# Spreading projected state-space inputs by DMA through DRAM instead of by identity matmuls, in a two-layer fp32 decoder trunk

## The chip, the cores and the metric

The kernel runs on one core of one Trainium2 chip. The metric is the device time of one execution in microseconds (us). Before the change three runs gave 1001.79, 1001.94 and 1002.18 us; the median is 1001.94 us.

## The reference

The input x is 256 tokens by 1024 channels, fp32. Two layers run one after the other, each a feed-forward block, a mixer and a second feed-forward block, then a final RMSNorm. The mixer of layer 0, the only part that the change touches, is a diagonal state-space model (S5):

```
u = (h @ w_in)                                # 256 tokens x 1024 channels
# 64 groups of 16 channels, each with a 64-dim complex diagonal state
bu = einsum('gph,tgh->tgp', b_bar, u);  s_t = lam_bar * s_(t-1) + bu_t
y  = Re(einsum('ghp,tgp->tgh', c, s)) + d_skip * u
z  = gelu(y);  val, gate = split(z @ w_out);  mixed = val * sigmoid(gate)
```

## The kernel before

Channels lie on the 128 partitions and the 256 tokens on the free axis. Every weight matrix comes as a stream of 326 units of 128 x 1024 numbers. SyncE (the queue SP) loads a unit into one of three `raw` slots (L313), once VectorE has finished with the unit three before it. ScalarE (ACT) rounds it to the high part `w_hi` (L364), VectorE (DVE) makes the low part `w_lo` (L803), in rings of four, and TensorE (PE) multiplies high by high, high by low and low by high (L1299 to L1301). The rounding of a unit waits, by `unit_done`, until PE has used the unit four before it. PE, ACT and DVE each follow an order written out by hand; nothing overtakes on an engine, and the engines meet by semaphores.

The S5 mixer starts with unit `b` of the stream (`b = S5_BASE`). Units b to b+7 project the input, one for every 128 channels, into the four PSUM banks of `acc`: bank q holds units 2q and 2q+1, 256 channels, and is called quarter q. The recurrence is not run token by token. The 256 tokens are cut into 64 chunks of 4 steps. For it the inputs have to lie with 4 steps x 32 channels (two groups, a pair) on the 128 partitions and with 8 pairs x 64 chunks on the free axis. That is the tile `u`, of which quarter q has 128 x 512 numbers. How one quarter runs:

- `inputs(q)`: ACT copies bank q from PSUM to the SBUF buffer `own_u` (L598), step-major. `own_u` has two halves, q even and q odd. ACT waits for the second unit of the quarter, and for q = 2 and 3 until PE has read the half that it overwrites.
- `s5_move(q)`: PE multiplies 16 blocks of 128 x 32 of the identity by `own_u` and so brings each step and each block of 32 channels to its partitions, back in bank q (L1617).
- `s5_scale_u(q)`: DVE multiplies bank q by the reciprocal RMS by steps, `rstd_step`, and writes `u` (L1052).
- `s5_inflow(q)`: PE multiplies `u` by the input matrices of the states, into the banks `gu` or `mx` (L1630).
- `s5_scan(q)`: DVE turns the inflow by tables (L1073 to L1079) and scans it over the chunks, real and imaginary part (L1082).
- `s5_state(q)`: DVE turns it back and writes the real part over `u` and the imaginary part to `state_im` (L1091 to L1101).
- `s5_own(q)`: PE computes what a chunk's inputs give in the chunk itself (L1638); `s5_outflow(q)`: PE adds what the states give (L1654). Then ACT applies gelu (L618), PE turns z back (L1663), and the output projection starts with `value_gate` (L1694).

In the code of the mixer, `project(k)` is the projection by unit b+k, and `split_after(n)` is the split of unit n+4: on ACT its rounding, on DVE its low part. The order of PE after unit 2 is: inflow(0), project(3), own(0), move(1), project(4), inflow(1), project(5), own(1), move(2), outflow(0), project(6), inflow(2), project(7), own(2), move(3), outflow(1), inflow(3), own(3), the turns of quarters 0 and 1, outflow(2), two corrections, value_gate parts, outflow(3). DVE runs scan(q), scale_u(q+1), state(q), with the low parts of two units after state(0), of one after state(1) and of none after state(2). ACT runs inputs(1), the roundings of b+7 and b+8, inputs(2), those of b+9 and b+10, inputs(3), that of b+11.

Of the kernel before, what the change touches and what calls it, by code (L numbers as in the profile page):

```python
# [62 lines left out]
CH = 2 * GROUP  # L63
STEPS = 4
CHUNKS = SEQ // STEPS
QUARTERS = 4
# [34 lines left out]
def trunk(nc, x_in, gains, last_gain, wstream, lam_re, lam_im, log_dt, b_re, b_im, c_re, c_im, skip, out):  # L101
    with ExitStack() as ctx:
# [3 lines left out]
        def sem(name):  # L106
            return ctx.enter_context(nc.semaphore(name))
# [112 lines left out]
        toep_act, toep_dve = sem("toep_act"), sem("toep_dve")  # L220
        rot_started, rot_ready, decay_ready = sem("rot_started"), sem("rot_ready"), sem("decay_ready")
        u_copied, u_moved, turned_back = sem("u_copied"), sem("u_moved"), sem("turned_back")
        rotated, unrotated, state_cleared = sem("rotated"), sem("unrotated"), sem("state_cleared")
        zeroed, skip_ready, own_done = sem("zeroed"), sem("skip_ready"), sem("own_done")
        u_ready, inflow_done, inflow_read = sem("u_ready"), sem("inflow_done"), sem("inflow_read")
# [72 lines left out]
        def last_turn(m, i):  # L298

            return isinstance(i, int) and i == TURNS - 1 and m == BODY - 1  # L300

        block = ctx.enter_context(nc.Block())

# [52 lines left out]
        def _(act):  # L356
# [9 lines left out]
            def split_after(done):  # L366

                if done + RING < UNITS:
                    n = done + RING
                    split_hi(n, n % RAW, n % RING)  # L370
# [219 lines left out]
            def s5_mixer():  # L590
                b = S5_BASE
                def inputs(q):
                    act.wait_ge(unit_done, b + 2 * q + 2)
                    if q == 0:
                        act.wait_ge(rot_ready, 1)
                    if q >= 2:
                        act.wait_ge(u_moved, q - 1)
                    act.activation(own_u[:, q % 2].rearrange("p t (j c) -> p t c j", j=STEPS),  # L598
                                   acc[:, q, :].rearrange("p (t c j) -> p t c j", t=2, j=STEPS),
                                   ACT.Copy).then_inc(u_copied, 1)  # L600

                inputs(0)
                root_by_steps(1)
# [1 line left out]
                split_after(b + 1)  # L605
                split_after(b + 2)
                inputs(1)
                split_after(b + 3)
                split_after(b + 4)
                inputs(2)  # L610
                split_after(b + 5)
                split_after(b + 6)
                inputs(3)
                split_after(b + 7)

                def gelu(q):
                    act.wait_ge(y_done, q + 1)
# [173 lines left out]
        def _(dve):  # L791
# [256 lines left out]

            def s5_scale_u(q):

                dve.wait_ge(u_moved, q + 1)
                dve.tensor_tensor(u[:, QP * q:QP * (q + 1), :], acc[:, q, :].rearrange("p (a c) -> p a c", a=QP),  # L1052
                                  rstd_step[:, :].unsqueeze(1).broadcast_to([P, QP, CHUNKS]),
                                  ALU.mult).then_inc(u_ready, 1)

# [237 lines left out]
        def _(pe):  # L1293
# [316 lines left out]
            def s5_move(q):  # L1610

                pe.wait_ge(u_copied, q + 1)
                for i in range(4):
                    for j in range(STEPS):
                        dst = acc[CH * j:CH * (j + 1), q, :].rearrange("p (t i c) -> p t i c", t=2, i=4)[:, :, i, :]
                        src = own_u[:, q % 2, :, CHUNKS * j:CHUNKS * (j + 1)]
                        mm = pe.matmul(dst, ident[:, CH * i:CH * (i + 1)], src, start=True, stop=True)  # L1617
                mm.then_inc(u_moved, 1)
# [81 lines left out]
            def s5_mixer():  # L1700
# [11 lines left out]
                s5_inflow(0)  # L1712
                project(3)
                s5_own(0)
                s5_move(1)
                project(4)
                s5_inflow(1)
                project(5)
                s5_own(1)
                s5_move(2)  # L1720
                s5_outflow(0)
                project(6)
                s5_inflow(2)
                project(7)
                s5_own(2)
                s5_move(3)
                s5_outflow(1)
                s5_inflow(3)
                s5_own(3)
# [471 lines left out]
```

## Time and profile before

| | |
|---|---|
| median of three runs | 1001.94 us |
| profiled execution, first to last instruction (span) | 999.6 us |
| what lies around the span, by the difference to the median | 2.3 us |
| PE busy | 987.1 us, 99% |
| DVE busy | 744.5 us, 74% |
| ACT busy | 571.2 us, 57% |
| moved by DMA | 172.57 MB, mean 173 GB/s |
| mean granted TensorE clock | 0.999 |

The page gives no other time for the profiled execution than its span; the difference to the median of the runs, 2.3 us, is taken as what lies around it. PE is the matmul engine; PEld in a row is its weight load, which overlaps. A queue's name with a q behind it (SPq, ACTq) is the issuing of DMAs by that engine. In the rows, `s_memory` is the block of SBUF that holds `u`, `own_u`, `state_im` and the tables, and `low_part` and `mx`, `gu`, `acc` are what the code calls them. A time in a timeline is microseconds from the span's start.

### The profile page before, as it was taken

The page shows a single profiled execution, that of the slowest core. Times are in us where ns is not written, and L with a number is a line of the kernel's source. Part 1 is how long each engine was busy: PE and PEld are TensorE (multiplying, and loading weights), DVE is VectorE, ACT ScalarE, POOL GpSimd, SP SyncE. Part 2 cuts the span into 40 slices and gives each one's busy share as a digit, 9 for nine tenths or more (in the row PEclk, how much of TensorE's full clock was granted, in tenths as well). Part 3 has the DMA queues.
Part 4 walks back from the last instruction along what each step waited for, and adds up shares of the span by engine and source line. Part 5 has one row for each costly group of instructions (what it writes and reads, how often), then busy time and mean ns, then how long its engine had stood idle before and what let it go on. Part 6 is the DMA issues. An engine that isn't in the chain of part 4 may idle for free.

```text
span 999.6 us, 19015 instructions
## 1 busy us (share of the span) xinstructions
PE 987.1 (99%) x7304; PEld 904.0 (90%) x7304; DVE 744.5 (74%) x922; ACT 571.2 (57%) x794; POOL 114.4 (11%) x144
## 2 busy tenths in 40 slices
PE   8999999999999999999999999999999999999997
PEld 8999999989999888888898888888899898888886
DVE  5789986889976777777687777776566587666666
ACT  7444447573365655555465555555599765555555
POOL 4854138100001000000010000001000010000000
PEclk9999999999999999999999999999999999999999
DMA  7555555443075565666646666566544256655563
GB/s 253 192 174 183 170 177 164 149 132 121 23 218 184 183 196 185 190 183 191 196 148 214 189 188 190 184 180 193 186 126 125 85 154 218 190 192 188 190 190 108
DMA packets 49049, 172.57 MB, mean 173 GB/s; under 512 B 6097, under 2 KB 6097, under 8 KB 48977
## 3 DMA queue, kind: packets, MB, share of 16 engines
q1 hardware_dynamic: 48544, 170.99, 54.3%
q8 instruction: 54, 0.88, 0.4%
q10 hardware_dynamic: 432, 0.55, 0.2%
q14 instruction: 19, 0.15, 0.0%
HBM read 170.47 MB, written 1.05 MB: 172 GB/s over the span
## 4 chain that ended last, share of the span: by engine, by line
PE 73%; DVE 13%; POOL 6%; ACT 4%; issue 4%; DMA 1%; SPq 0%; DVEq 0%; POOLq 0%; ACTq 0%
PE mx L1314 11%; PE gu L1314 11%; PE mx L1317 6%; PE gu L1317 6%; PE acc L1356 4%; PE gu L1299 4%; PE gu L1300 4%; PE gu L1301 4%; DVE w_lo L803 4%; PE acc L1360 2%; PE gu L1356 2%; PE mx L1356 2%; PE acc L1343 2%; PE acc L1345 2%; PE acc L1347 2%
## 5 line engine op out<-in xcount | busy, mean ns | idle before, releaser
L803 DVE TENSOR_TENSOR w_lo<-raw,w_hi 128x1024 fp32r<-128x1024 f32 x258 | 324.3, 1266 | 91.0 <-ACT w_hi L364 90.4
L364 ACT ACTIVATE w_hi<-raw 128x1024 fp32r<-128x1024 f32 x259 | 270.5, 1052 | 80.8 <-DMA raw<-wstream_dram 22.3
L1299 PE MATMUL gu<-g,w_hi 128*128 128x256 f32 x560 | 161.4, 288 | 1.5 <-DVE g L943 1.3
L1300 PE MATMUL gu<-g,w_hi 128*128 128x256 f32 x560 | 158.4, 283 | 0.0
L1301 PE MATMUL gu<-g,w_lo 128*128 128x256 f32 x560 | 158.4, 283 | 0.0
L1314 PE MATMUL mx<-g,w_hi 128*128 128x512 f32 x480 | 119.9, 392 | 0.0
L1314 PE MATMUL gu<-g,w_hi 128*128 128x512 f32 x464 | 116.2, 392 | 0.0
L1299 PEld LDWEIGHTS gu<-g,w_hi 128*128 128x128 f32 x560 | 107.3, 192 | 2.3 <-issue 1.5
L1300 PEld LDWEIGHTS gu<-g,w_hi 128*128 128x128 f32 x560 | 107.4, 192 | 0.1
L1301 PEld LDWEIGHTS gu<-g,w_lo 128*128 128x128 f32 x560 | 107.3, 192 | 0.0
L1314 PEld LDWEIGHTS mx<-g,w_hi 128*128 128x128 f32 x480 | 87.0, 189 | 16.0
L1314 PEld LDWEIGHTS gu<-g,w_hi 128*128 128x128 f32 x464 | 83.8, 188 | 15.6
L374 ACT ACTIVATE tmp<-tmp 128x256 f32<-128x256 f32 x68 | 28.4, 418 | 108.8 <-DVE tmp L813 86.6
L1940 POOL TENSOR_TENSOR ssq<-ssq,tmp 128x512 f32<-128x512 f32 x12 | 18.5, 1538 | 583.6 <-ACT tmp L510 583.6
L877 DVE TENSOR_TENSOR w_lo<-raw,w_hi 128x1024 fp32r<-128x1024 f32 x58 | 70.8, 1223 | 16.2 <-ACT w_hi L479 16.2
L1317 PEld LDWEIGHTS mx<-g,w_lo 128*128 128x128 f32 x480 | 65.5, 190 | 4.7
L1317 PEld LDWEIGHTS gu<-g,w_lo 128*128 128x128 f32 x464 | 63.2, 190 | 4.7
L1317 PE MATMUL mx<-g,w_lo 128*128 128x256 f32 x480 | 66.9, 282 | 0.0
L479 ACT ACTIVATE w_hi<-raw 128x1024 fp32r<-128x1024 f32 x57 | 60.0, 1053 | 11.1 <-PE mx L1317 5.1
L1317 PE MATMUL gu<-g,w_lo 128*128 128x256 f32 x464 | 64.6, 282 | 0.0
L820 DVE TENSOR_TENSOR tmp<-tmp 128x256 f32<-128x256 f32 x88 | 40.5, 460 | 12.3 <-ACT tmp L374 11.6
L1299 PE MATMUL acc<-h_hi,w_hi 128*128 128x256 f32 x168 | 48.4, 288 | 0.1
(309 smaller groups left out, 1927.1 us busy)
## 6 DMA issues: line engine op xcount, KB each, us to landing
raw<-wstream_dram SPq DMA_DIRECT2D x318, 512.0 KB, 3.7
x<-x_in_dram SPq DMA_DIRECT2D x4, 256.0 KB, 5.9
raw<-wstream_dram SPq DMA_DIRECT2D x3, 256.0 KB, 5.7
out_dram<-x_tok SPq DMA_DIRECT2D x3, 256.0 KB, 2.0
gain_row<-last_gain_dram SPq DMA_DIRECT2D x1, 512.0 KB, 4.4
raw<-wstream_dram ACTq DMA_DIRECT2D x1, 256.0 KB, 4.6
s_memory<-b_re_dram SPq DMA_DIRECT2D x1, 256.0 KB, 4.6
s_memory<-b_im_dram SPq DMA_DIRECT2D x1, 256.0 KB, 5.2
```

The source lines that it names most:

```text
L364: act.activation(weights(unit)[0], raw[:, s_raw, :], ACT.Copy).then_inc(hi_ready, 1)
L374: act.activation(tmp[:, f % 2, 2, :], tmp[:, f % 2, 0, :], ACT.Silu).then_inc(silu_ready, 1)
L479: act.activation(w_hi[:, n0 % RING, :], raw[:, n0 % RAW, :], ACT.Copy).then_inc(hi_ready, 1)
L803: dve.tensor_tensor(lo, raw[:, n % RAW, :], hi.bitcast(F32), ALU.subtract).then_inc(lo_ready, 1)
L820: dve.tensor_tensor(tmp[:, m, 3, :], tmp[:, m, 2, :], tmp[:, m, 1, :], ALU.mult).then_inc(h_ready, 1)
L877: dve.tensor_tensor(w_lo[:, n0 % RING, :], raw[:, n0 % RAW, :], w_hi[:, n0 % RING, :].bitcast(F32), ALU.subtract).then_inc(lo_ready, 1)
L1299: pe.matmul(dst, a, hi, start=start, stop=False, skip_group_check=check)
L1300: pe.matmul(dst, a, lo, start=False, stop=False, skip_group_check=check)
L1301: return pe.matmul(dst, b_, hi, start=False, stop=stop, skip_group_check=check)
L1314: pe.matmul(bank.rearrange("p (r t) -> p r t", r=2), w_hi[:, s, P * kb:P * kb + P], g_both[:, :, kb, :], start=kb == 0, stop=False, skip_g ...
L1317: last = pe.matmul(bank[:, 0:SEQ], w_lo[:, s, P * kb:P * kb + P], g_hi[:, kb, :], start=False, stop=kb == KB - 1, skip_group_check=True)
L1356: pe.matmul(kept_bank(d).rearrange("p (i t) -> p i t", i=2), w_hi[:, s, at:at + P], h_kept[:, 2 * p + r, :, :], start=p == 0 and r == 0, s ...
```

## The change

Quarter 0 stays as it is. For quarters 1, 2 and 3 the identity matmuls (`s5_move`) go. ACT, after its copy to `own_u`, issues four DMAs that write 32 partitions each to a DRAM scratch `u_dram` (64 KB each, in runs of 64 numbers, 256 bytes). Two roundings later (one, in quarter 3) it waits until all four have landed (`u_stored`), and issues one DMA that reads the quarter back (256 KB, 128 rows of 2 KB) straight into `u`. DVE then waits for that DMA (`u_spread`) and multiplies `u` in place, from SBUF instead of from PSUM. The wait before `inputs(3)` is for the stores of quarter 1; that before `inputs(2)` stays a wait on PE's move of quarter 0.

```diff
+        u_dram = nc.dram_tensor("u_dram", (QUARTERS, STEPS, CH, 2, 4, CHUNKS), F32, kind="Internal").ap()
@@ scalar engine, s5_mixer
                     act.wait_ge(unit_done, b + 2 * q + 2)
                     if q == 0:
                         act.wait_ge(rot_ready, 1)
-                    if q >= 2:
-                        act.wait_ge(u_moved, q - 1)
+                    if q == 2:
+                        act.wait_ge(u_moved, 1)
+                    if q == 3:
+                        act.wait_ge(u_stored[1], 16 * 4)
+                def store_inputs(q):
+                    act.wait_ge(u_copied, q + 1)
+                    for i in range(4):
+                        rows = slice(CH * i, CH * (i + 1))
+                        act.dma_start(u_dram[q, :, :, :, i, :].rearrange("j h t c -> h t j c"),
+                                      own_u[rows, q % 2].rearrange("p t (j c) -> p t j c", j=STEPS)).then_inc(
+                            u_stored[q], 16)
+
+                def spread_inputs(q):
+                    act.wait_ge(u_stored[q], 16 * 4)
+                    act.dma_start(u[:, QP * q:QP * (q + 1), :].rearrange("p a c -> p (a c)"),
+                                  u_dram[q].rearrange("j h t i c -> (j h) (t i c)")).then_inc(u_spread[q], 16)
                 inputs(1)
+                store_inputs(1)
                 split_after(b + 3)
                 split_after(b + 4)
+                spread_inputs(1)
                 inputs(2)
+                store_inputs(2)
                 split_after(b + 5)
                 split_after(b + 6)
+                spread_inputs(2)
                 inputs(3)
+                store_inputs(3)
                 split_after(b + 7)
+                spread_inputs(3)
@@ vector engine
             def s5_scale_u(q):
-                dve.wait_ge(u_moved, q + 1)
-                dve.tensor_tensor(u[:, QP * q:QP * (q + 1), :], acc[:, q, :].rearrange("p (a c) -> p a c", a=QP),
+                mine = u[:, QP * q:QP * (q + 1), :]
+                if q:
+                    dve.wait_ge(u_spread[q], 16)
+                else:
+                    dve.wait_ge(u_moved, 1)
+                dve.tensor_tensor(mine, mine if q else acc[:, q, :].rearrange("p (a c) -> p a c", a=QP),
                                   rstd_step[:, :].unsqueeze(1).broadcast_to([P, QP, CHUNKS]),
@@ tensor engine, s5_mixer
                 s5_own(0)
-                s5_move(1)
                 project(4)
                 s5_inflow(1)
                 project(5)
                 s5_own(1)
-                s5_move(2)
                 s5_outflow(0)
                 project(6)
                 s5_inflow(2)
                 project(7)
                 s5_own(2)
-                s5_move(3)
                 s5_outflow(1)
```

## Rows read from the trace of the kernel before

**Rows 1.** Page, part 1: busy time (share of the span) and instructions.

```profile
PE 987.1 (99%) x7304; PEld 904.0 (90%) x7304; DVE 744.5 (74%) x922; ACT 571.2 (57%) x794; POOL 114.4 (11%) x144
```

**Rows 2.** Waits of PE, longest first: total us, times, longest us.

```profile
PE gu L1299 <- DVE g L943: 1.3, 1, 1.3
```

**Rows 3.** Windows: length, busy us by engine, granted clock, DMA share, GB/s.

```profile
229.28:273.03 43.75, 43.09 (x642) 40.04 (x642) 43.42 (x59) 15.30 (x18) 0.00 (x0) 1.00 0.18 59
```

**Rows 4.** Chain that ended last, in the S5 mixer: start us, us, what.

```profile
258.81 0.59 DVE s_memory L1052
...
259.45 2.09 PE mx L1630 x64
...
273.24 1.95 PE acc L1654 x32
```

**Rows 5.** Source line L1617, the moves: duration ns min/median/max, first and last start.

```profile
L1617 PE MATMUL acc<-s_memory,ident x128: 272/273/297, 224.5 to 257.1; 128*32 128x128 f32 x128
```

**Rows 6.** Timeline of PE: start us, us, line, operation [idle before <-releaser].

```profile
232.22 1.09 PE L1638 MATMUL acc<-s_memory 128*64 128x128 f32 x16
233.49 1.08 PE L1617 MATMUL acc<-s_memory,ident 128*32 128x128 f32 x32 [0.17 <-ACT s_memory L598]
...
234.50 0.39 PE L1299 MATMUL acc<-g,w_hi 128*128 128x256 f32 x1
...
237.56 0.34 PE L1630 MATMUL mx<-s_memory,low_part 128*64 128x64 f32 x4
...
249.91 0.34 PE L1630 MATMUL gu<-s_memory,low_part 128*64 128x64 f32 x4
...
257.27 2.02 PE L1654 MATMUL acc<-s_memory 128*64 128x128 f32 x32
```

**Rows 7.** Timeline of ACT, the copies (L598) and roundings (L364).

```profile
232.33 1.10 ACT L598 ACTIVATE s_memory<-acc 128x512 f32<-128x512 f32 x1 [1.02 <-PE acc L1301]
...
237.72 1.06 ACT L364 ACTIVATE w_hi<-raw 128x1024 fp32r<-128x1024 f32 x1 [3.43 <-PE acc L1301]
242.74 1.10 ACT L598 ACTIVATE s_memory<-acc 128x512 f32<-128x512 f32 x1 [3.96 <-PE acc L1301]
...
250.08 1.06 ACT L364 ACTIVATE w_hi<-raw 128x1024 fp32r<-128x1024 f32 x1 [4.13 <-PE acc L1301]
255.10 1.10 ACT L598 ACTIVATE s_memory<-acc 128x512 f32<-128x512 f32 x1 [3.96 <-PE acc L1301]
256.49 1.06 ACT L364 ACTIVATE w_hi<-raw 128x1024 fp32r<-128x1024 f32 x1 [0.29 <-DMA raw<-wstream_dram]
```

**Rows 8.** Timeline of DVE: the first multiply into u, the last state.

```profile
235.06 0.67 DVE L1052 TENSOR_TENSOR s_memory<-acc,rstd_step 128x512 f32<-128x512 f32 x1
...
272.35 0.68 DVE L1101 TENSOR_TENSOR s_memory<-tmp 128x504 f32<-128x504 f32 x1
```

**Rows 9.** Page, part 6, DMA issues: count, KB each, median us to landing.

```profile
raw<-wstream_dram SPq DMA_DIRECT2D x318, 512.0 KB, 3.7
...
out_dram<-x_tok SPq DMA_DIRECT2D x3, 256.0 KB, 2.0
...
s_memory<-b_re_dram SPq DMA_DIRECT2D x1, 256.0 KB, 4.6
```

**Rows 10.** Source lines L748 and L331: what one DMA issue takes, ns min/median/max.

```profile
L748 ACTq DMA_DIRECT2D raw<-wstream_dram x1: 450/450/450, 1.3 to 1.3; - x1
...
L331 SPq DMA_DIRECT2D par<-lam_im_dram x1: 712/712/712, 5.3 to 5.3; - x1
```

**Rows 11.** Source line L324, three 256 KB loads at the kernel's start: issue, landing.

```profile
L324 SPq DMA_DIRECT2D raw<-wstream_dram x3: 388/432/432, 0.8 to 3.1; - x3
...
DMA to landing us min/median/max: 2.8/5.7/6.6
```

**Rows 12.** Windows at the kernel's end, columns as in Rows 3.

```profile
993.00:994.00 1.00, 0.61 (x3) 0.19 (x1) 0.93 (x4) 0.91 (x3) 0.00 (x0) 1.00 0.00 0
...
997.00:998.00 1.00, 0.00 (x0) 0.00 (x0) 0.00 (x0) 0.00 (x0) 0.00 (x0) 0.69 0.70 272
```

More of the change, by code:

```diff
@@ L222, in trunk @@
         u_copied, u_moved, turned_back = sem("u_copied"), sem("u_moved"), sem("turned_back")
+        u_stored = [sem(f"u_stored{q}") for q in range(QUARTERS)]
+        u_spread = [sem(f"u_spread{q}") for q in range(QUARTERS)]
         rotated, unrotated, state_cleared = sem("rotated"), sem("unrotated"), sem("state_cleared")
```

## The prediction, made before the changed kernel ran

> **What bounds the kernel now.** I read the page's busy shares first. PE is busy 987.1 of 999.6 us [rows 1], and the longest wait of any PE group is 1.3 us [rows 2]. So elsewhere in the kernel nothing that is late in the mixer can be made good: what the mixer loses, the kernel loses. The change touches only the stretch from about 232 to 260 us, and the windows show that from 229.28 to 273.03, 43.75 us, PE is busy 43.09 and DVE 43.42 us [rows 3]. Two engines are full at once, at the full clock (1.00, the 2.4 GHz level), so a saving on one alone is worth next to nothing. Which of them sets the end the chain tells: it runs through DVE up to the multiply into `u` of quarter 3 at 258.81, and only then over inflow(3) at 259.45 to outflow(3) at 273.24 [rows 4]. DVE's last state write ends at 273.03 [rows 8], 0.2 us before outflow(3) starts. Both routes meet there.
>
> **What goes.** Each move is 32 matmul records that start within about 1 us [rows 5, 6]. With the wait for ACT's copy before it, it costs more: own(0) starts at 232.22 and project(4) at 234.50 [rows 6], 2.28 us, of which own itself takes about 1.0 (1.09 with the drain of its last matmul). So each move is worth 1.3 us of PE's time, three 3.9 us. DVE saves nothing: it multiplies the same 128 x 512 numbers; from SBUF instead of PSUM I take the same 0.67 us [rows 8].
>
> **What comes.** Per quarter ACT issues five DMAs, and the inputs make two trips one after the other, each with its landing waited for.
> - One issue: 0.45 us on ACT's queue [rows 10], 0.71 us for the slowest of small rows [rows 10]. I take 0.45, the row of the same queue: four stores hold ACT 1.8 us, and the last starts 1.35 us after the first.
> - A store's landing: 256 KB in 2 KB rows to DRAM land in 2.0 us [rows 9]. The new ones are a quarter of that in 256-byte runs; bounds 1.5 (fewer bytes; three quarters of that row) and 3.5 us (near the 3.7 of a 512 KB load [rows 9]). I take 2.0.
> - The read back, 256 KB: the quickest load of this size landed in 2.8 us [rows 11], one among other loads took 4.6 [rows 9], and a store of the size 2.0 [rows 9]. The DMA engines are at 0.18 in this stretch [rows 3] and the weight queue is held up by DVE's late splits, so I take 2.8; bounds 2.0 and 4.2 (short of the 4.6, which stood in a row of loads).
>
> On DMA: Bandwidth & Descriptors (Specifications) in the Trainium skill speaks against the change: below 512 bytes a transfer is read, modified and written. No row of this trace shows a store in such runs. If it brought the landing to the 3.5 us bound, two of the three quarters would wait longer, by 2.6 us in all.
>
> Nothing else hides in the edit: the wait of `inputs(3)` on the stores of quarter 1 has long been met, and PE and DVE issue no DMA.
>
> **The sum, quarter by quarter.** Queued behind the new wait on DVE are state(q-1), the low parts and scan(q); behind ACT's wait for the stores is the next `inputs`; PE sits in inflow(q).
> - Quarter 1. The copy ends at 233.43 [rows 7]. Stores are issued from 233.55 to 235.35 and landed at 236.9. ACT then rounds b+7 until 236.35. Project(4) runs 1.3 us earlier, so the rounding of b+8, at 237.72 before [rows 7], is free to start at 236.4 and ends at 237.4. The read back is issued there and lands at 240.2; DVE multiplies until 240.9, against a start at 235.06 before [rows 8]; inflow(1) starts at 241.0 against 237.56 [rows 6]: 3.45 us late. PE, finished with project(4) at 236.15, is idle for 4.85 us.
> - Quarter 2. From inflow(1) to the copy of quarter 2 it is 242.74 - 237.56 = 5.2 us [rows 6, 7], so that copy starts at 246.2. The stores land at 250.7, but in front of the read back stands the rounding of b+10, which waits for project(6): 250.08 - 237.56 = 12.5 us after inflow(1) [rows 6, 7], 11.2 without the move. That is 252.2; rounded at 253.2, read back issued at 253.3, landed at 256.1, multiplied at 256.8. inflow(2) starts at 256.85 against 249.91 [rows 6]: 6.95 late, after 4.85 us of idle PE.
> - Quarter 3. The copy follows 5.2 us after inflow(2) [rows 6, 7]: 262.05 to 263.15. Last store issued 264.6, landed 266.6; the rounding of b+11 waits for its load as it did before [rows 7] and ends at the same time, 266.6. Read back issued 266.7, landed 269.5, multiplied 270.25; inflow(3) at 270.3 against 259.45 [rows 4]: 10.85 late. PE ends outflow(1) about 264.9 (2.02 us from 257.27 before [rows 6], shifted by 6.95 and less the last move), so it idles 5.4 us.
> - After it. inflow(3) to outflow(3) was 13.8 us of full PE [rows 4], and stays so: 284.1. By DVE: multiply at 269.6, then state(2), scan(3), state(3), 273.03 - 258.81 = 14.2 us before [rows 4, 8], gives 283.8. Both routes end 10.8 us late.
>
> So without a change of the clock the span goes to 999.6 + 10.85 = 1010.4, and with the 2.3 us around it the time to 1012.8. The check: 15.1 us of new idle PE less 3.9 of moves is 11.2.
>
> **The clock.** PE is idle three times for about 5 us. The only such stretch in the trace is the end: PE stops in 993 to 994 (0.61 us busy), and in 997 to 998 the granted clock is 0.69 of full [rows 12], that is, it fell to the 1.2 GHz level after some 4 us without a matmul. My three gaps are 0.8 to 1.3 us longer than that. One sample says that a fall can come in each, not that it must; I give each a chance a little under even, 1.3 falls of three. What follows the gap, an inflow of 2.1 us and a projection of 2.9, would take twice as long at the lower level until it rises: up to 4.9 us more, 2.5 if it rises halfway. I take 2.4 per fall, and 1.3 of them: 3.2 us. The three gaps stay on the path to the next copy, so this adds in full.
>
> On the clock, TensorE: Matmul & The Clock Gate (Why this matters for your kernels) in the Trainium skill warns against idle gaps between bursts of matmuls, after which the array is back at half rate. The row of the end agrees; by that rule alone all three gaps would cost, 7.2 us instead of 3.2.
>
> Forecast: 1012.8 + 3.2 = 1016.0 us.
>
> **The rivals.**
> - The clock stays up: 1012.8. For it: the gaps exceed the one sample by only about a microsecond. Range 1010 to 1015 with the bounds of the read back.
> - Dear transfers: store at 3.5 (+2.6) and read back at 4.2 (+1.4 each, 4.2), with two falls: 1012.8 + 6.8 + 4.8 = 1024.4. For it: short runs and small rows have no price in this trace. Against it: the DMA engines are nearly free here.
> - The transfers are hidden, no change: 1001.9. It would need copy end to multiply within what there is now, 235.06 - 233.43 = 1.6 us in quarter 1 [rows 7, 8], where one landing alone is 2.0. Even then DVE's full queue keeps the end.
> - Faster: PE, not DVE, is what the end hangs on. Then the 3.9 us of moves come back: 998.0. It decides where a quarter's two trips fit in 1.6 us and DVE gives up 3.9 us that it doesn't give in rows 3. Both speak against it.
>
> **How the numbers follow.** Forecast (chain exposed, one or two falls) 0.50; clock stays up 0.27; dear transfers or three falls 0.17; hidden 0.03; faster 0.03. The range is 1010.5 to 1023.0: below it lie the two last rivals and a read back of 2.0 us, above it the far end of the dear case. Slower by over 0.2% (2 us, about what a measurement of this kernel can tell from no change) is 0.50 + 0.27 + 0.17 = 0.94, within it 0.03, faster 0.03.
>
> **What would show it.** In the profile after: DVE's multiply L1052 (its line after) waiting for the read-back DMA three times, by about 5.1, 3.5 and 2.2 us; inflow idle before by 4.9, 4.9 and 5.4 us; five issues per quarter on ACTq at 0.45; landings of 2.0 and 2.8 us; granted clock below 1.00 somewhere in 240 to 280; nothing lost or won after the mixer. I am wrong if ACT's issues or the short runs cost twice what I take, or if DVE waits but PE makes it good from other work.

## The result

| | before | after |
|---|---|---|
| median of five runs | 1001.94 us | 1018.97 us |
| lowest and highest | 1001.44, 1002.55 | 1015.86, 1022.58 |
| profiled execution, span | 999.6 us | 1014.1 us |
| mean granted clock of the profiled execution | 0.999 | 0.994 |

The ratio is 1.0168, with a 95% interval of 1.0149 to 1.0187: the kernel became 17 us slower. Forecast were 1016.0 us and a range of 1010.5 to 1023.0. Two things are worth reading in the table. The profiled execution, at 1015.86 us, is the quickest of the five, so its trace shows less of the loss than the median has. And the five runs lie 6.7 us apart, where those of before lie 1.1 us apart. The mean granted clocks of the five are 0.994, 0.993, 0.992, 0.990 and 0.988 in the order of their times, quickest first: 6 us of missing clock (0.006 of 1017 us) between the ends, for 6.7 us of time. (Five runs are few for a spread: 21 later runs of the kernel before lay 3.0 us apart.)

The page of after, busy shares and DMA issues (KB each, median us to landing):

```profile
PE 989.0 (98%) x7208; PEld 906.8 (89%) x7208; DVE 745.1 (73%) x922; ACT 571.5 (56%) x794; POOL 114.4 (11%) x144
...
u_dram<-s_memory ACTq DMA_DIRECT2D x12, 64.0 KB, 2.3
s_memory<-u_dram ACTq DMA_DIRECT2D x3, 256.0 KB, 2.5
```

PE has 96 instructions less than in [rows 1] and 1.9 us more of busy time, since a matmul at the lower clock is busy for longer: inflow(1) took 3.59 us in the chain of after, an inflow at the full clock 2.09 [rows 4]. DVE and ACT do the same work as before. What is new is waiting. The waits of after in the stretch 225 to 300 us, longest first (total us, times, longest us):

```profile
DVE s_memory L1081 <- DMA s_memory<-u_dram: 12.6, 3, 5.4
PEld mx L1659 <- DVE s_memory L1081: 11.1, 2, 6.0
PE mx L1659 <- DVE s_memory L1081: 10.7, 2, 5.7
...
PE gu L1659 <- DVE s_memory L1081: 3.3, 1, 3.3
```

L1081 is the multiply into `u`, L1052 before; L1659 is the inflow, L1630 before. DVE waits three times for the read-back, 12.6 us in all, and behind it PE waits 14.0 us. The timeline of ACT and its queue in after (start us, us):

```profile
232.33 1.10 ACT L604 ACTIVATE s_memory<-acc 128x512 f32<-128x512 f32 x1 [2.78 <-PE acc L1330]
233.46 3.09 ACTq L612 DMA_DIRECT2D u_dram<-s_memory  x4
236.65 2.00 ACT L368 ACTIVATE w_hi<-raw 128x1024 fp32r<-128x1024 f32 x2 [3.22 <-PE acc L1330]
238.04 0.35 ACTq L618 DMA_DIRECT2D s_memory<-u_dram  x1
248.02 1.10 ACT L604 ACTIVATE s_memory<-acc 128x512 f32<-128x512 f32 x1 [9.38 <-PE acc L1330]
249.16 3.06 ACTq L612 DMA_DIRECT2D u_dram<-s_memory  x4
252.32 1.06 ACT L368 ACTIVATE w_hi<-raw 128x1024 fp32r<-128x1024 f32 x1 [3.19 <-issue]
253.97 1.06 ACT L368 ACTIVATE w_hi<-raw 128x1024 fp32r<-128x1024 f32 x1 [0.59 <-PE acc L1330]
253.99 0.33 ACTq L618 DMA_DIRECT2D s_memory<-u_dram  x1
263.88 1.11 ACT L604 ACTIVATE s_memory<-acc 128x512 f32<-128x512 f32 x1 [8.85 <-PE acc L1330]
265.02 2.56 ACTq L612 DMA_DIRECT2D u_dram<-s_memory  x4
```

The first copy starts at the very time of [rows 7]. One trip round is a copy (1.1 us), four issues (3.1), the landing, one issue, another landing, the multiply, inflow, project, and the next copy. Before, the copies came 10.4 and 12.4 us after each other [rows 7], now 15.7 and 15.9. The multiplies on DVE in after, and its last state write:

```profile
240.58 0.69 DVE L1081 TENSOR_TENSOR s_memory<-s_memory,rstd_step 128x512 f32<-128x512 f32 x1 [5.43 <-DMA s_memory<-u_dram]
256.46 0.69 DVE L1081 TENSOR_TENSOR s_memory<-s_memory,rstd_step 128x512 f32<-128x512 f32 x1 [3.37 <-DMA s_memory<-u_dram]
271.64 0.69 DVE L1081 TENSOR_TENSOR s_memory<-s_memory,rstd_step 128x512 f32<-128x512 f32 x1 [3.79 <-DMA s_memory<-u_dram]
...
285.29 0.69 DVE L1130 TENSOR_TENSOR s_memory<-tmp 128x504 f32<-128x504 f32 x1
```

and outflow(3) in the timeline of PE:

```profile
287.47 2.02 PE L1683 MATMUL acc<-s_memory 128*64 128x128 f32 x32
```

DVE's last state write begins at 285.29 against 272.35 [rows 8], 12.94 us late, and 12.6 of that are the three waits. On PE outflow(3) begins at 287.47; in the chain of after it stands at 287.54, 14.3 us after its place in the chain of before [rows 4]. So PE is 1.4 us later than DVE is. Before, outflow(3) followed 0.2 us behind the end of DVE's last state write, now 1.6 us behind it (285.98 to 287.54): from inflow(3) to outflow(3) PE takes 15.2 us (272.38 to 287.54), where it took 13.8 before [rows 4]. From outflow(3) on almost nothing is lost or won: the spans differ by 14.5 us. Windows of after (columns as in [rows 3]) show where the 1.4 us come from:

```profile
240.00:242.00 2.00, 0.67 (x12) 0.68 (x14) 1.42 (x2) 0.00 (x0) 0.00 (x0) 0.82 0.06 22
242.00:244.00 2.00, 2.00 (x44) 2.00 (x42) 1.99 (x5) 0.00 (x0) 0.00 (x0) 0.50 0.00 0
244.00:246.00 2.00, 2.00 (x29) 1.93 (x26) 1.97 (x3) 0.00 (x0) 0.00 (x0) 0.83 0.00 0
...
258.00:260.00 2.00, 2.00 (x47) 1.88 (x41) 1.99 (x5) 0.00 (x0) 0.00 (x0) 0.59 0.00 0
260.00:262.00 2.00, 2.00 (x10) 2.00 (x11) 1.97 (x4) 0.00 (x0) 0.00 (x0) 0.56 0.04 8
...
272.00:274.00 2.00, 1.61 (x30) 1.62 (x32) 1.99 (x4) 0.00 (x0) 0.00 (x0) 0.50 0.00 0
274.00:276.00 2.00, 2.00 (x48) 2.00 (x46) 1.97 (x4) 0.00 (x0) 0.00 (x0) 0.65 0.01 4
```

Behind each of PE's three gaps, of 4.9, 3.3 and 5.7 us, the granted clock is at the 1.2 GHz level for a while. The missing share of it comes to 1.7 us each time (0.36 + 1.00 + 0.34 in the first), 5.1 us in all. The last of the three stands between inflow(3) and outflow(3), and is what makes that stretch 1.4 us longer. Not all of the 5.1 us is time lost: a fall costs only where nothing else is waited for.

### The profile page after: what moved, and what is told of

The parts are those of the page before. It is cut to its first block, busy times and chain, and to the rows that moved or that the text cites. A ratio compares the mean times of both kernels' runs of the same rounds, so it can differ in the third digit from the quotient of the medians.

```text
span 1014.1 us, 18838 instructions
## 1 busy us (share of the span) xinstructions
PE 989.0 (98%) x7208; PEld 906.8 (89%) x7208; DVE 745.1 (73%) x922; ACT 571.5 (56%) x794; POOL 114.4 (11%) x144
## 4 chain that ended last, share of the span: by engine, by line
PE 81%; DVE 7%; POOL 3%; ACT 3%; issue 2%; DMA 1%; ACTq 0%; SPq 0%; DVEq 0%; POOLq 0%
PE mx L1343 11%; PE gu L1343 11%; PE mx L1346 6%; PE gu L1346 5%; PE gu L1328 5%; PE gu L1330 5%; PE gu L1329 5%; PE acc L1385 4%; DVE w_lo L828 3%; PE acc L1389 2%; PE gu L1385 2%; PE mx L1385 2%; PE acc L1372 2%; PE acc L1374 2%; PE acc L1376 2%
```

## The experiments

Each kernel was timed beside runs of the kernel before on the same chip, and the ratios are against those. My theory was a chain: DVE's full queue sets the end of the stretch, so what DVE waits for the two landings is lost one for one, and to that comes the clock that falls in PE's gaps. (An idle-time matmul, or filler, below is a matmul whose result nobody reads.)

**One quarter alone.** The change for quarter 1; quarters 2 and 3 are moved by PE as before.

```diff
-                store_inputs(2)
-                spread_inputs(2)
-                store_inputs(3)
-                spread_inputs(3)
                 s5_own(1)
+                s5_move(2)
...
                 s5_own(2)
+                s5_move(3)
```

> The change for quarter 1 alone; quarters 2 and 3 are moved by PE as before. Theory (VectorE's queue is the bound, so its wait is lost one for one and PE's slack beside it is not): VectorE waits 5.4 us once and is full from there on, and the time is 5.4 to 6.5 us above the kernel before, about 1007.5 us. Rival (PE's lateness counts, 3.5 us in quarter 1 less what PE has saved): 1004.5 to 1005.5 us.

Measured: 1007.82 us, ratio 1.0054 (1.0039 to 1.0070), 5.7 us above the median of before beside it. The multiplies on DVE in this kernel:

```profile
241.09 0.69 DVE L1077 TENSOR_TENSOR s_memory<-s_memory,rstd_step 128x512 f32<-128x512 f32 x1 [5.84 <-DMA s_memory<-u_dram]
253.52 0.67 DVE L1077 TENSOR_TENSOR s_memory<-acc,rstd_step 128x512 f32<-128x512 f32 x1
264.79 0.67 DVE L1077 TENSOR_TENSOR s_memory<-acc,rstd_step 128x512 f32<-128x512 f32 x1
```

One wait of 5.84 us, none for a DMA after it, and the time is up by 5.7. PE's lateness in that quarter, less by what it saved, would have been smaller, so the rival as it stands fell. The time alone does not shut out PE, though: the granted clock in this kernel is 0.59 and 0.56 from 240 to 248 us, 3.4 us of missing clock, and PE's wait of 5.4 us, less the move and with a part of that, comes out near 5.7 too. What shows that the wait of DVE is lost is DVE's own timeline, where the last state write begins at 278.42, 6.1 us late; outflow(3) can't run before it.

**No moves, and nothing in their place.**

```diff
                 s5_own(0)
-                s5_move(1)
...
-                dve.wait_ge(u_moved, q + 1)
+                if q:
+                    dve.wait_ge(u_copied, q + 1)
+                else:
+                    dve.wait_ge(u_moved, 1)
```

> The kernel before without the identity matmuls of quarters 1 to 3 and with no DMA in their place: VectorE multiplies the bank as the projection left it, after ScalarE's copy. This leaves out the spreading of three quarters, so the numbers that it computes are others; only the time is of use. It is the change with transfers that cost nothing. Theory (VectorE's full queue sets the end of the stretch): three moves are 3.9 us of PE, but PE then waits in front of outflow(3), and the time is 1001.0 to 1002.0 us, at most 1 us less than before. Rival (PE sets the end): 998.0 us.

Measured: 1002.67 us, ratio 1.0003 (0.9993 to 1.0012). That is 0.7 us above the range of the theory, and far from the rival's 998.0. The 3.9 us of PE work that the change takes away are worth nothing, even with transfers that cost nothing. I had expected the wait in front of outflow(3); it stands in front of inflow(3), the longest wait of PE in this kernel (total us, times, longest us):

```profile
PE mx L1633 <- DVE s_memory L1055: 3.3, 1, 3.3
```

and in the window behind it (columns as in [rows 3]):

```profile
260.00:264.00 4.00, 4.00 (x76) 3.95 (x72) 3.85 (x7) 0.55 (x2) 0.00 (x0) 0.57 0.02 6
```

PE waits in front of inflow(3) for what it has saved, and behind that wait the clock is at 0.57 for 4 us. That is 1.7 us of clock lost by doing less work, and here it costs time: DVE's last state write is only 0.2 us late (272.56), outflow(3) 1.8 us (274.95 against 273.17 in PE's timeline). Only this execution has a trace; by their mean clocks it happened in half of the ten runs: five have 0.995 or 0.996 and took 1002.95 to 1004.84 us, the others 0.999 or 1.000 and 1001.18 to 1002.39. Even the five runs at the full clock have a median only 0.3 us below that of the kernel before beside them (1002.42).

**The DMAs beside the moves, read by nobody.**

```diff
+                    if q > 1:
+                        act.wait_ge(u_spread[q - 1], 16)
-                    act.dma_start(u[:, QP * q:QP * (q + 1), :].rearrange("p a c -> p (a c)"),
+                    act.dma_start(h_lo[:, :, :].rearrange("p k t -> p (k t)").bitcast(F32),
...
                 norm_block(2, KB - 1)
+                act.wait_ge(u_spread[3], 16)
```

> The kernel before with its moves, and beside them all the DMAs of the change: ScalarE issues the twelve stores and the three read-backs at the places of the change, but the read-backs go to a tile that nobody reads, and VectorE multiplies the moved bank as before. It prices the issues, ScalarE's wait for the stores and the traffic by themselves. Theory (only VectorE's wait for the landing costs): 1001.9 to 1003 us. Rival (ScalarE's queue, held for 2.5 to 3.1 us by the issues and longer by the wait for the stores, makes roundings late, or the short runs slow the weight stream): 1005 us or more.

Measured: 1004.95 us, ratio 1.0022 (1.0013 to 1.0032). That is 2.2 us by the ratio and 2.5 by the medians, above the theory's 1003 and just short of the rival's 1005: the theory fell, and the rival's cause, ACT's held queue, is seen, though not at the roundings. DVE's last state write is on time in this kernel (272.46). But ACT's queue holds the first gelus behind the stores of quarter 3. The timeline of ACT in this kernel (start us, us):

```profile
256.35 3.75 ACTq L612 DMA_DIRECT2D u_dram<-s_memory  x4
...
261.58 0.33 ACTq L620 DMA_DIRECT2D h_lo<-u_dram  x1
261.94 1.28 ACT L645 ACT_TABLE_LOAD   x1 [0.69 <-DMA u_dram<-s_memory]
263.24 1.09 ACT L645 ACTIVATE s_memory<-acc 128x512 f32<-128x512 f32 x2
```

and PE's own timeline at that place:

```profile
263.89 1.14 PE L1691 MATMUL acc<-ident,s_memory 128*128 128x128 f32 x8 [1.37 <-ACT s_memory L645]
```

PE stands 1.4 us before it can turn z, in a stretch where it was full. In the changed kernel this does not show: the inflow of quarter 3 is later still, and nothing waits for the gelus there.

The rest need not be the price of the DMAs. The edit has one wait more, at the end of the mixer, and behind it ACT's next table load comes late (timeline of ACT):

```profile
325.16 1.28 ACT L392 ACT_TABLE_LOAD   x1 [4.34 <-issue]
```

In the kernel before, this table load starts as soon as ACT's last activation of the mixer ends (at 319.37). The read-back that the new wait is for had been issued at 261.58, so why the load is late is not shown. PE then waits 1.9 us in all for DVE's `h_kept`, which it never does in the kernel before. The profiled execution is one of the slower ones (1005.91), and its outflow(3) is 1.6 us late of 4.5 us in the span. So 2.2 us is an upper bound for the traffic and the issues; 1.4 of it has a place in the trace.

**PE kept busy in the gaps.**

```diff
+            def s5_fill(q, n):
+
+                pe.wait_ge(neg_ready, 1)
+                if q >= 2:
+                    pe.wait_ge(inflow_read, q - 1)
+                for _ in range(n):
+                    pe.matmul((gu, mx)[q % 2][:, 0, 0:SEQ], neg_ident[:, :], g_hi[:, 0, :], start=True, stop=True,
+                              skip_group_check=True)
...
                 project(4)
+                s5_fill(1, 38)
                 s5_inflow(1)
...
                 project(6)
+                s5_fill(2, 24)
                 s5_inflow(2)
...
                 s5_outflow(1)
+                s5_fill(3, 44)
                 s5_inflow(3)
```

> The changed kernel, with idle-time matmuls on PE in front of inflow(1), inflow(2) and inflow(3): 38, 24 and 44 matmuls of 128x256 at 0.118 us each, into the PSUM bank that the inflow overwrites. They give PE work for 4.5, 2.8 and 5.2 us of the waits and change nothing else. Theory (the loss is made of a chain of DMA trips, and of the clock that falls in the gaps): the granted clock stays at 1.00, the three stretches of 3.4 us at the lower level go, each worth 1.7 us of PE work, and the time is about 1011 us (1018.97 before; the profiled execution of 1015.86 less 5), with runs that lie closer together than the 6.7 us of the changed kernel. Rival (the clock costs nothing on the path, the scatter has another source such as the DMAs): 1015 to 1019, scatter as before. Second rival (the fillers run past the landing of the inputs and delay the inflow): above 1019.

Measured: 1015.53 us, 1013.93 to 1016.34, ratio 1.0131 (1.0116 to 1.0147). The scatter shrinks from 6.7 us in five runs to 2.4 in four, and the time by 3.4 us by the medians, 3.7 by the ratios, whose intervals do not touch; so the clock does cost, but the 1011 us that I expected are missed by 4.5. Windows around quarter 2 in this kernel:

```profile
252.00:256.00 4.00, 3.63 (x31) 3.43 (x30) 1.57 (x2) 1.06 (x1) 0.00 (x0) 1.00 0.38 109
256.00:260.00 4.00, 2.71 (x70) 2.64 (x71) 3.45 (x6) 0.00 (x0) 0.00 (x0) 1.00 0.02 6
```

and the timeline of ACT and its queue there:

```profile
246.98 1.11 ACT L604 ACTIVATE s_memory<-acc 128x512 f32<-128x512 f32 x1 [7.91 <-PE acc L1330]
...
253.19 1.06 ACT L368 ACTIVATE w_hi<-raw 128x1024 fp32r<-128x1024 f32 x1 [1.33 <-DMA raw<-wstream_dram]
254.00 0.33 ACTq L618 DMA_DIRECT2D s_memory<-u_dram  x1
```

The clock stays at 1.00 and the copy of quarter 2 comes 1 us sooner than in the changed kernel, yet its read-back is issued at 254.00, as before at 253.99. The gain was taken within one quarter by something that the clock doesn't drive. Two candidates stand in these rows: the rounding in front of the read-back, which waits for its weight load, or the stores' own landing. The four stores of quarter 2 decide it for this execution (source line L612, window 240 to 258; ns, then us to landing):

```profile
L612 ACTq DMA_DIRECT2D u_dram<-s_memory x4: 577/630/649, 248.1 to 250.1; - x4
DMA to landing us min/median/max: 3.6/3.9/4.0
```

The rounding began at 253.19, so it was out of the way; the last store was issued at 250.1 and took 3.9 us to land, which is 254.0. In the changed kernel the same four took 2.5 to 2.8 us.

With the clock at 1.00 this kernel is also the cleanest sight of the bound: DVE waits 11.8 us for the read-backs, its last state write is 12.5 us late (284.87), so is outflow(3) (285.67 in PE's timeline), and the span is 12.5 us longer than before.

**The read-back in front of the roundings**, in the changed kernel and together with the fillers.

```diff
                 store_inputs(2)
+                spread_inputs(2)
                 split_after(b + 5)
                 split_after(b + 6)
-                spread_inputs(2)
```

> The changed kernel with one thing moved: on ScalarE the read-back of a quarter is issued as soon as its four stores have landed, in front of the one or two roundings of weight units instead of behind them. Theory (the landing of the stores comes last anyway: they are issued over 2.6 to 3.1 us and land 2.1 to 2.3 us after the last issue): nothing gained, within 1 us of the changed kernel, 1017 to 1020 us. Rival (my prediction's step for quarter 2, that the rounding which waits for project(6) holds the read-back): 2 to 3 us less, 1015 to 1017 us.

> The changed kernel with both edits: idle-time matmuls on PE in the three gaps, and the read-back issued ahead of the roundings. In the profile with the fillers alone the copy of quarter 2 came 1 us earlier than in the changed kernel, but the read-back was issued at the same time, because the rounding in front of it waited for its weight load. Theory (what the steady clock gave was taken by the order of ScalarE's queue): with both, 1 to 2 us less than with the fillers alone, 1013.5 to 1014.5 us. Rival (the stores land that late by themselves, since the weight load runs beside them): as with the fillers alone, 1015 to 1016 us.

Measured: without fillers 1017.32 us, ratio 1.0154 (1.0141 to 1.0168), an interval that overlaps that of the changed kernel; with fillers 1014.99 us, ratio 1.0127 (1.0112 to 1.0143), against 1.0131 without the move. Neither differs from its partner by more than the intervals allow. Both runs moved the read-back in all three quarters (the cut shows quarter 2). The stores of quarter 2 in the first of these kernels say why (timeline of ACT and its queue):

```profile
249.34 2.58 ACTq L612 DMA_DIRECT2D u_dram<-s_memory  x4
255.39 0.33 ACTq L618 DMA_DIRECT2D s_memory<-u_dram  x1
```

The read-back is issued as soon as the stores allow, and the slowest of them takes 4.1 us from its issue to its landing (the median of this quarter is 2.7); with fillers the four take 4.0 to 4.1. So what took the gain of the clock is the landing of the stores, not the order of ACT's queue; the theory that both edits together win fell, its rival holds. A weight load of 512 KB is in flight beside these stores (issued at 247.9 in the first kernel, landed 6.7 us later); in quarter 3 of that kernel, where the load issued at 263.9 had landed before the last store was issued at 268.4, all four take 2.1. So late landings go together with loads in flight in these traces; no run separates the two.

**Short runs in the loads instead of in the stores.**

```diff
-        u_dram = nc.dram_tensor("u_dram", (QUARTERS, STEPS, CH, 2, 4, CHUNKS), F32, kind="Internal").ap()
+        u_dram = nc.dram_tensor("u_dram", (QUARTERS, P, 2, STEPS, CHUNKS), F32, kind="Internal").ap()
...
+                    act.dma_start(u_dram[q].rearrange("p t j c -> p (t j c)"),
+                                  own_u[:, q % 2].rearrange("p t n -> p (t n)")).then_inc(u_stored[q], 16)
...
+                    for j in range(STEPS):
+                        act.dma_start(
+                            u[CH * j:CH * (j + 1), QP * q:QP * (q + 1), :].rearrange("p (t i) c -> p t i c", t=2),
+                            u_dram[q].rearrange("(i h) t j c -> j h t i c", i=4)[j]).then_inc(u_spread[q], 16)
```

> The changed kernel with the short runs moved from the stores to the loads: one store per quarter writes the copy as it lies, 128 rows of 2 KB, and four loads of 32 partitions read it back in runs of 256 bytes. Bytes, trips and waits are the same. Theory (what counts is two landings one after the other and five issues on one queue, wherever the short runs are): four issues of 0.6 to 0.7 us now stand behind the wait for the store instead of in front of it, and the time is that of the changed kernel, 1016 to 1021 us. Rival (stores in runs below 512 bytes are dear in themselves, loads are not): the store lands sooner by 1 us or more and the chain gets shorter by 1 us a quarter, 1013 to 1016 us.

Measured: 1020.79 us, ratio 1.0180 (1.0166 to 1.0194). Its DMA issues:

```profile
u_dram<-s_memory ACTq DMA_DIRECT2D x3, 256.0 KB, 2.9
s_memory<-u_dram ACTq DMA_DIRECT2D x12, 64.0 KB, 2.3
```

The time is within the theory's range, and the rival (the store lands 1 us sooner, 1013 to 1016 us) fell. A store of 256 KB in 2 KB rows landed in 2.9 us at the median, a quarter of the bytes in 256-byte runs in 2.3 in the page of after: the short writes are not what is dear. The long rows do not land early in quarter 2 either: that store took 3.8 us, the one of quarter 3 2.0. The Trainium skill says, in DMA: Bandwidth & Descriptors (Specifications), that transfers below 512 bytes are read, modified and written. Whether that happened no trace here can show; a cost of it is not seen in the landings. What is dear is the issuing. One plain store or load is issued in 0.33 to 0.35 us, a DMA of 32 partitions and 256 runs in 0.58 to 1.07 in the changed kernel.

**Work put over the trips.** Three kernels with the projections ahead of the inflows. The first sends all three quarters by DMA, the second only quarters 2 and 3 (quarter 1 is moved by PE, and DVE keeps its order, the last three lines of the cut), the third adds 20 idle-time matmuls to the second in front of inflow(3). The read-backs of quarters 1 and 2, where they are, stand one rounding earlier.

```diff
                 project(4)
-                s5_inflow(1)
                 project(5)
+                s5_inflow(1)
                 s5_own(1)
                 s5_outflow(0)
                 project(6)
-                s5_inflow(2)
                 project(7)
+                s5_inflow(2)
...
-                s5_scale_u(1)
                 s5_state(0)
+                s5_scale_u(1)
```

> All three quarters by DMA as in the change, but with work put over the trips: PE runs project(5) before inflow(1) and project(7) before inflow(2), so that the copies of quarters 2 and 3 and their trips start early; VectorE runs state(0) before it multiplies quarter 1; the read-back stands one rounding earlier. Theory (the loss was the exposed trips alone): VectorE waits only once, 1.6 to 2 us for quarter 1, and the time is 1003 to 1006 us. Rival (the DMAs cost something besides VectorE's wait, or the gaps of PE only move and the clock still falls): 1008 us or more.

> As the reordered kernel, but only quarters 2 and 3 go by DMA; quarter 1 is moved by PE as before and VectorE keeps its order. Theory: no wait of VectorE is left, two moves (2.6 us of PE) are gone, VectorE's full queue still sets the end, and the time is that of the kernel before, 1001.5 to 1003.5 us; what PE saves stands as a wait in front of inflow(3), where the clock can fall as it did with no moves at all. Rival: PE's saving is worth something, 999.5 us.

> The same with 20 idle-time matmuls (2.4 us) on PE in front of inflow(3). Theory: the granted clock stays at 1.00 there, and the time is 0.5 to 1 us below the one without them and nowhere below the kernel before by more than 0.5 us: 1001 to 1002.5 us. Rival (the wait in front of inflow(3) is harmless): no difference between the two.

Measured: 1010.60 us, ratio 1.0083 (1.0069 to 1.0097); 1007.86 us, ratio 1.0061 (1.0048 to 1.0075); 1008.24 us, ratio 1.0060 (1.0046 to 1.0074). The first wins back half of the loss, but all three theories are missed by 4 to 6 us. The first one's rival, 1008 us or more, holds; the third is no quicker than the second, as its rival says, though its fillers did not cover the wait. DVE's waits for the read-back had indeed shrunk to 3.6 and 2.8 us. What I had not seen stands in the timeline of ACT and its queue, here of the second kernel:

```profile
253.64 3.09 ACTq L610 DMA_DIRECT2D u_dram<-s_memory  x4
261.20 1.06 ACT L368 ACTIVATE w_hi<-raw 128x1024 fp32r<-128x1024 f32 x1 [7.59 <-DMA raw<-wstream_dram]
261.21 0.33 ACTq L616 DMA_DIRECT2D s_memory<-u_dram  x1
```

Now that the copies come early, the rounding in front of the read-back waits 7.6 us for a weight load, and the read-back with it. The stores before it had landed by 258.2 (the last issued at 256.1, 2.1 us), so here it was the order that held the read-back, for 3.0 us. The PE gap in front of inflow(3) had grown to 6.3 us, more than 20 fillers cover, and the clock fell in both kernels (0.80 from 256 to 264 and 0.77 from 264 to 272 in the second, 0.92 and 0.65 in the third).

**The same, mended.** Read-backs ahead of the roundings, 50 fillers in front of inflow(3).

> The kernel with two quarters by DMA and work over the trips, mended at the two places that its profile shows: the read-backs are issued ahead of the roundings that waited for weight loads, and 50 idle-time matmuls instead of 20 stand in front of inflow(3). Theory (nothing but exposed landings and the clock made it slow): VectorE's waits shrink below 1 us in all and the time is 1002 to 1004 us. Rival (the stores land late beside the weight loads, 3.4 us in that profile, so quarter 2 stays exposed by 2 us): 1005 to 1007 us. Neither is below the kernel before.

Measured: 1006.48 us, ratio 1.0045 (1.0032 to 1.0059), and the rival holds. The granted clock is 1.00 from 252 to 276 us, so nothing of the 4.4 us is the clock. Quarter 3 is hidden, quarter 2 is not, as DVE's timeline shows:

```profile
251.81 0.69 DVE L1077 TENSOR_TENSOR s_memory<-s_memory,rstd_step 128x512 f32<-128x512 f32 x1 [3.15 <-DMA s_memory<-u_dram]
263.11 0.67 DVE L1077 TENSOR_TENSOR s_memory<-s_memory,rstd_step 128x512 f32<-128x512 f32 x1
```

**Quarter 3 alone, hidden.** PE moves quarters 1 and 2, project(7) runs before inflow(2), and the read-back goes ahead of the rounding.

```diff
                 project(6)
-                s5_inflow(2)
                 project(7)
+                s5_inflow(2)
                 s5_own(2)
...
                 store_inputs(3)
+                spread_inputs(3)
                 split_after(b + 7)
-                spread_inputs(3)
```

> The change for quarter 3 alone, with its trips hidden: quarters 1 and 2 are moved by PE, project(7) runs before inflow(2), so that the copy of quarter 3 comes 3 us before its place in the kernel before, and the read-back is issued ahead of the rounding. In the kernel with two quarters by DMA this quarter's inputs lay ready 3 us before VectorE asked for them. Theory (a hidden transfer is worth nothing, since VectorE's full queue and not PE sets the end; its exposed time is all that it costs): VectorE waits 0 to 1 us, the time is that of the kernel before, 1001.5 to 1003.5 us. Rival (PE's move was worth its 1.3 us): 1000.5 to 1001 us. Second rival (ScalarE's held queue makes the gelus late, as with the DMAs that nobody reads): 1004 us.

Measured: 1005.49 us, ratio 1.0034 (1.0022 to 1.0045). The theory is missed by 2 us, and both rivals lie below what was measured. DVE never waits for a DMA in it, and still it waits, as its timeline shows:

```profile
255.36 1.22 DVE L1096 TENSOR_TENSOR tmp<-gu,s_memory 128x1024 f32<-128x1024 f32 x1 [1.89 <-PE gu L1653]
261.29 0.69 DVE L1075 TENSOR_TENSOR s_memory<-s_memory,rstd_step 128x512 f32<-128x512 f32 x1
```

and the window in which PE waits for it:

```profile
260.00:266.00 6.00, 3.97 (x74) 3.97 (x76) 5.80 (x10) 2.53 (x4) 0.00 (x0) 0.72 0.11 38
```

Putting project(7) in front of inflow(2) to start the trip early makes scan(2) wait 1.89 us for the inflow, and PE, ahead of DVE after that, waits 4.0 us in front of inflow(3), where the clock falls again. The trip is hidden, and making room for it costs 3.6 us by the medians. The new order was not run without the DMAs, so how much of that is the order's alone is not shown. No kernel here that sends inputs by DMA is as quick as the one before.

## Why the prediction was right, and where its terms were off

- **The bound.** Held, as long as the clock is up. With the moves gone and no transfers the ratio is 1.0003 (0.9993 to 1.0012); with the gaps filled DVE waits 11.8 us and everything is 12.5 us late. Where the clock falls behind the last gap it is PE that reaches outflow(3) last: 1.4 us behind DVE's lateness in the changed kernel. The check by PE's account comes out as well: 14.0 us of new waits less 3.9 of moves is 10.1, and 4.2 of the 5.1 us of missing clock bring it to 14.3.
- **The issues.** Mis-sized. I took 0.45 us each, 1.8 for four stores, by the row of a load of 128 rows [rows 10]; they took 3.1, 3.1 and 2.6 us. The last store starts 2.5, 2.0 and 1.9 us after the first instead of 1.35, which makes a quarter 0.6 to 1.1 us longer wherever the stores come last. The upper row, 0.71, was the better neighbour.
- **The landings.** The last stores of quarters 1 and 3 landed in 2.1 us (taken: 2.0), the read-backs in 2.4 to 2.5 (taken: 2.8); both errors are small and opposed. The stores of quarter 2 took 2.5 to 2.8 us in the changed kernel, and up to 4.1 in its variants. I had called the DMA engines free by their mean share over 44 us, 0.18 [rows 3]; while these stores run, from 248 to 252 us, it is 0.77 in the changed kernel, their own bytes included.
- **Quarter 1.** Multiply at 240.58, forecast 240.2 to 240.25; inflow(1) at 241.33, forecast 241.0. Right to 0.4 us by two errors that cancel: the stores landed at 238.0 (forecast 236.9), behind the roundings instead of in front of them, and the read-back took 0.3 us less.
- **Quarter 2.** Multiply at 256.46, forecast 256.1; inflow(2) at 257.21, forecast 256.85. Right to 0.4 us, and that is luck. The copy came at 248.02, 1.8 us later than forecast (246.2), since inflow(1) and project(5) ran in part at the lower clock. I let the read-back wait for the rounding behind project(6), and it did: the rounding begins at 253.97, the read-back at 253.99. But it waited for the rounding's start and not, as I had it, for its end 1.1 us later, and the landing was 0.4 us shorter; these two made up for most of PE's lateness. The stores, which I had landed at 250.7, landed at about 253.6 (the last issued at 251.1, 2.5 us). So the order that I blamed held the read-back by 0.3 us only, and with the rounding out of the way the time doesn't measurably change. It did hold it where the copies came early.
- **Quarter 3.** Multiply at 271.64, forecast 269.6; inflow(3) at 272.38, forecast 270.3. Of these 2.1 us 1.8 stand already at the copy (263.88, forecast 262.05): 0.4 come from quarter 2, and from inflow(2) to the copy PE takes 6.7 us where I took 5.2, by the clock that falls behind gap 2. The longer issues add 0.6, the quicker read-back takes 0.3 off.
- **The waits.** DVE waited 5.4, 3.4 and 3.8 us for the read-backs, forecast 5.1, 3.5 and 2.2; PE stood 4.9, 3.3 and 5.7 us, forecast 4.9, 4.9 and 5.4. Gap 2 is shorter than forecast because project(6), at the end of a stretch that the clock had slowed, came later.
- **The clock.** I gave 1.3 falls of 2.4 us each, 3.2 us. (1.3 times 2.4 is 3.1.) The profiled run has three, with 1.7 us of missing clock each. That they add in full did not hold: the first is swallowed by gap 2, as inflow(2) is only 0.4 us late; the second costs 1.5 us up to the copy of quarter 3, the third 1.4 on the way to outflow(3), 2.9 us together. Filling the gaps gives 3.4 us back at the median (1.0168 to 1.0131), and 1.9 between the two profiled runs (1015.86 and 1013.93), each the quickest of its kernel. So the size was about right by luck: more falls, each smaller, one of them free. The Trainium skill's warning about idle gaps, in TensorE: Matmul & The Clock Gate (Why this matters for your kernels), held for all three gaps of this run; that all three falls would cost in full, 7.2 us, did not.
- **The sum.** Forecast 1012.8 without falls and 1016.0 with them. The kernel with its gaps filled, whose clock stays at 1.00 in the mixer, has 1015.5: the chain was undersized by about 2.5 us at the median, and by 1.7 in its profiled run (span 1012.1 against 1010.4). The issues and the landings of quarter 2 are of that size; I have not separated them. The forecast case, an exposed chain and falls of the clock, is the one that came, 3 us dearer.
- **The ranges.** For the rival whose clock stays up I gave 1010 to 1015 with the bounds of the read-back. The upper bound of 4.2 us, 1.4 more in each of three quarters, makes 1017.0.
- **After the mixer.** As forecast, nothing was won back: 14.3 us late at outflow(3), 14.5 in the span.

Open is how the falls beyond the three of the profiled run come about in the slower runs; only their mean clocks are known. Two ways round the losses were not tried: issuing the DMAs from another queue than ACT's, and one trip from SBUF to SBUF instead of two through DRAM.

## What to carry to other kernels

Before an engine's work is handed to another resource, ask what sits in series, not how busy the engine is: PE was 99% busy here, and taking 3.9 us from it was worth nothing, since DVE was as full in the same stretch and set the end. A trip through DRAM costs two landings of 2 to 3 us and its issues one after the other, 6.7 to 7.3 us from the end of the copy to the multiply here, so it pays only where that time lies free between producer and consumer; here there were 1.6 to 3.6 us. And when a kernel lives at the full clock, price each new wait of TensorE twice, once as a wait and once as a fall of the clock that can come behind it.

## What the hardware showed that I had not expected

- Less work on TensorE can cost clock: with the moves gone and nothing else changed, a wait of 3.3 us in front of inflow(3) was followed by a granted clock of 0.57 over 4 us in the traced run. Half of the ten runs have a mean clock as low as this run's.
- One DMA issue on ACT's queue took 0.33 to 0.35 us for plain rows, and 0.58 to 1.07 us for 32 partitions of eight 256-byte runs each.
- Stores of 64 KB in 256-byte runs to DRAM landed in 2.3 us at the median of the changed kernel, while 256 KB in 2 KB rows took 2.9 us. In quarter 2, the same stores took up to 4.1 us in the variants, with a weight load in flight, and the one with 2 KB rows 3.8.
